# Weight-quarter sums of the up blocks moved from GpSimd to VectorE in a two-layer decoder step

## The reference

```
h2 = rmsnorm(x, g_ffn)                       # 544 x 1024
u, gt = jnp.split(h2 @ w_up, 2, axis=-1)     # 544 x 2816 each
u_ext = jnp.concatenate([conv_buf, u], axis=1)
acc = b_conv
for k in range(CONV_W):                      # CONV_W = 3
    acc = acc + w_conv[k] * u_ext[:, k:k + T]
x = x + (jax.nn.gelu(acc) * gt) @ w_down     # 2816 -> 1024
```

## Time and profile before

| | |
|---|---|
| time, median of 3 runs | 2200.66 us (2198.23 to 2205.04) |
| time of the profiled execution | 2216.76 us |
| its span, first to last instruction | 2214.9 us |
| TensorE matmuls | 2160.3 us busy, 98% |
| VectorE | 1065.3 us busy, 48% |
| ScalarE | 501.3 us busy, 23% |
| GpSimd | 495.9 us busy, 22% |
| mean granted TensorE clock | 0.992 of full |
| DMA | 237.52 MB, 107 GB/s mean |

### The profile page before, as it was taken

The page is one execution under the profiler, slowest core; times in us unless marked ns, Lnnn a source line. Parts: engine busy times, 40 slices in busy tenths (PEclk is TensorE's granted clock), DMA queues, the critical chain, the costliest instruction groups (busy, mean ns, idle before and its releaser), DMA issues.

```text
span 2214.9 us, 30179 instructions
## 1 busy us (share of the span) xinstructions
PE 2160.3 (98%) x12119; PEld 1732.5 (78%) x12119; DVE 1065.3 (48%) x2228; ACT 501.3 (23%) x1076; POOL 495.9 (22%) x501
## 2 busy tenths in 40 slices
PE   8998999999999999999999989999999999999999
PEld 7787866778887888888877867767788878888887
DVE  5466646554115555543326666465441265555522
ACT  3124124432011222210112231354220212222100
POOL 5140010001002443444331300100100034444442
PEclk9999999999999999999999999999999999999999
DMA  5674541112221222222283736210122212222222
GB/s 155 233 249 166 218 153 39 39 41 98 76 80 57 88 84 76 89 78 80 66 286 113 269 120 246 97 39 20 60 98 80 73 60 77 94 77 79 77 85 73
DMA packets 172302, 237.52 MB, mean 107 GB/s; under 512 B 39551, under 2 KB 151680, under 8 KB 169408
## 3 DMA queue, kind: packets, MB, share of 16 engines
q1 hardware_dynamic: 153320, 133.11, 19.6%
q0 software_dynamic: 18400, 102.36, 12.5%
q10 hardware_dynamic: 444, 0.12, 0.0%
HBM read 222.76 MB, written 21.11 MB: 110 GB/s over the span
## 4 chain that ended last, share of the span: by engine, by line
PE 90%; DVE 4%; ACT 2%; DMA 2%; issue 1%; another core or an unknown queue 1%; POOL 0%; DVEq 0%; SPq 0%; ACTq 0%; POOLq 0%
PE PS L918 36%; PE PS L863 27%; PE PS L1029 5%; PE PS L885 4%; PE PS L911 3%; PE PS L1363 2%; PE PS L1280 2%; PE PS L1291 2%; PE PS L429 2%; DMA arena<-in_cache_kv_slc_dram,idx 2%; ACT arena L1574 1%; PE PS L1238 1%; DVE arena L2263 1%; PE PS L1263 1%
## 5 line engine op out<-in xcount | busy, mean ns | idle before, releaser
L863 PE MATMUL PS<-hT,ring 128*128 128x272 f32 x1792 | 425.9, 397 | 5.7 <-issue 2.4
L863 PEld LDWEIGHTS PS<-hT,ring 128*128 128x128 f32 x1792 | 341.5, 192 | 84.7 <-issue 15.2
L1574 ACT ACTIVATE arena<-PS 128x272 f32<-128x272 f32 (+12 forms) x426 | 173.5, 432 | 816.2 <-PE PS L918 221.7
L918 PE MATMUL PS<-arena,ring 128*128 128x272 f32 x1232 | 303.1, 393 | 0.9 <-DVE xT L1932 0.6
L1932 DVE TENSOR_TENSOR arena<-PS,arena 128x272 f32<-128x272 f32 (+4 forms) x204 | 98.7, 493 | 365.4 <-PE PS L918 189.6
L918 PEld LDWEIGHTS PS<-arena,ring 128*128 128x128 f32 x1232 | 233.8, 190 | 49.6 <-issue 1.7
L918 PE MATMUL PS<-arena,kv_kT 128*128 128x272 f32 x912 | 224.3, 395 | 4.4 <-ACT arena L1574 4.4
L815 POOL TENSOR_TENSOR kv_kT<-ring 128x512 f32<-128x512 f32 (+1 forms) x64 | 82.8, 1293 | 607.5 <-PE PS L918 454.9
L1932 DVE TENSOR_TENSOR xT<-PS,xT 128x272 f32<-128x272 f32 (+1 forms) x184 | 85.8, 466 | 267.0 <-PE PS L918 183.5
L918 PEld LDWEIGHTS PS<-arena,kv_kT 128*128 128x128 f32 x912 | 174.2, 191 | 41.3 <-ACT arena L1574 5.3
L863 PE MATMUL PS<-arena,ring 128*128 128x272 f32 x768 | 177.2, 393 | 3.2 <-DVE arena L1932 3.2
(11 more groups left out here) (337 smaller groups left out, 2480.3 us busy)
## 6 DMA issues: line engine op xcount, KB each, us to landing
ring<-in_w_up_dram SPq DMA_DIRECT2D x88, 512.0 KB, 4.5
ring<-in_w_in_dram SPq DMA_DIRECT2D x68, 512.0 KB, 4.5
ring<-in_w_down_dram SPq DMA_DIRECT2D x32, 512.0 KB, 4.4
arena<-in_state_kv_win_dram POOLq DMA_DIRECT2D x4, 2048.0 KB
ring<-in_w_out_dram SPq DMA_DIRECT2D x16, 512.0 KB, 4.0
out_dram<-in_state_kv_win_dram POOLq DMA_DIRECT2D x2, 4064.0 KB, 39.8
ring<-in_w_down_dram SPq DMA_DIRECT2D x16, 384.0 KB, 3.5
ring<-in_w_in_dram SPq DMA_DIRECT2D x16, 256.0 KB, 4.8
```

Source lines behind the costliest of these rows:

```text
L863: mm = pe.matmul(PS[0:m, b + a, 0:HALF], weight(k), rhs(k)[:, HALF * a:HALF * a + HALF], start=(k == 0), stop=(k == nk - 1))
L918: mm = pe.matmul(PS[:, bank, 0:HALF], weight[:, k, :], rhs(k), start=(start and k == 0), stop=(stop and k == kc - 1), skip_group_check=not ...
L1574: return nc.scalar.activation(out, in_, func, **kw)
```

## The change

The sums of u1 to u10 are made by VectorE, in a function of the same four instructions; GpSimd keeps those of g1 to g10 and d0 to d11. The new sums count on a semaphore of their own, `u_sum`, for which TensorE waits in the u blocks. On VectorE the sums of u1 stand after the three copies and ahead of `conv(0)`; those of u_(i+1) stand after `conv(c + 1)` of block i, ahead of the token sums and of the adds of g_i.

```diff
+OTHERS = [name for name in SEVENS if name[0] != "u"]
...
+        def w_summed(eng, name, step):
+
+            if name[0] == "u":
+                return S.at(eng, "u_sum", 4 * int(name[1:]) - 4 + step)
+            return S.at(eng, "w_sum", 4 * OTHERS.index(name) + step)
...
-                for name in SEVENS:
+                for name in OTHERS:
                     weight_sums(name)
...
-                pe.wait_ge(*S.at(pe, "w_sum", 4 * n + 1))
+                pe.wait_ge(*w_summed(pe, name, 1))
...
+                def weight_sums(name):
+
+                    n, s = SEVEN_AT[name], wslot(name)[0]
+                    new = sums[n % 2]
+                    if n >= 2:
+                        dv.wait_ge(*S.filled(dv, last_ticket(SEVENS[n - 2])))
+                    dv.wait_ge(*w_landed(dv, name))
+                    tt(new[:, 0], quarter(s, 4, 0, 1), quarter(s, 4, 1, 1), ALU.add).then_inc(*S.inc(dv, "u_sum"))
+                    tt(quarter(s, 4, 0, 1), quarter(s, 4, 0, 0), quarter(s, 4, 0, 1), ALU.subtract).then_inc(*S.inc(dv, "u_sum"))
+                    dv.wait_ge(*w_summed(dv, name, 1))
+                    tt(new[:, 1], new[:, 0], quarter(s, 4, 0, 0), ALU.subtract).then_inc(*S.inc(dv, "u_sum"))
+                    dv.wait_ge(*w_summed(dv, name, 3))
+                    tt(new[:, 2], quarter(s, 4, 1, 0), new[:, 1], ALU.subtract).then_inc(*S.inc(dv, "u_sum"))
...
+                weight_sums("u1")
                 for c in range(2):
                     conv(c)
...
                     conv(c)
                     conv(c + 1)
+                    if i + 1 < FFN // WCOLS:
+                        weight_sums(f"u{i + 1}")
                     if 4 <= i < 8:
                         for step in range(4):
                             token_sum(i - 4, step)
```

More of the change, by code:

```diff
@@ L815, in weight_sums @@
                     gp.tensor_tensor(new[:, 0], quarter(s, kc, 0, 1), quarter(s, kc, 1, 1), ALU.add).then_inc(*S.inc(gp, "w_sum"))
-                    gp.wait_ge(*S.at(gp, "w_sum", 4 * n + 1))
+                    gp.wait_ge(*w_summed(gp, name, 1))
                     gp.tensor_tensor(quarter(s, kc, 0, 1), quarter(s, kc, 0, 0), quarter(s, kc, 0, 1), ALU.subtract).then_inc(*S.inc(gp, "w_sum"))
                     gp.tensor_tensor(new[:, 1], new[:, 0], quarter(s, kc, 0, 0), ALU.subtract).then_inc(*S.inc(gp, "w_sum"))
-                    gp.wait_ge(*S.at(gp, "w_sum", 4 * n + 3))
+                    gp.wait_ge(*w_summed(gp, name, 3))
                     gp.tensor_tensor(new[:, 2], quarter(s, kc, 1, 0), new[:, 1], ALU.subtract).then_inc(*S.inc(gp, "w_sum"))
-                for name in SEVENS:
+                for name in OTHERS:
                     weight_sums(name)
@@ L933, in seven_products @@
                 pe.wait_ge(*taken[0])
-                pe.wait_ge(*S.at(pe, "w_sum", 4 * n + 3))
+                pe.wait_ge(*w_summed(pe, name, 3))
                 pe.wait_ge(*t2[0])
@@ L941, in seven_products @@
                 pe.wait_ge(*taken[1])
-                pe.wait_ge(*S.at(pe, "w_sum", 4 * n + 4))
+                pe.wait_ge(*w_summed(pe, name, 4))
                 half_product(z, new[:, 2], right, kc, False, True).then_inc(*S.fill(pe, second))
```

## The result

| | before | changed |
|---|---|---|
| median | 2201.45 us (2197.51 to 2205.04, 20 runs) | 2207.72 us (2201.61 to 2213.82, 20 runs) |
| ratio | | 1.0034, 95% interval 1.0026 to 1.0042 |
| span of the profiled execution | 2214.9 us | 2210.8 us |
| VectorE busy | 1065.3 us | 1046.1 us |
| GpSimd busy | 495.9 us | 379.6 us |

The changed kernel is slower by 6.3 us. VectorE got 80 instructions more and is busy 19 us less.

The account below looks back on a forecast made before the run. TensorE was taken to bound blocks u1 to g10. Head delay 5.2 us plus clock 1.7 us gave 6.9 us, on the median of 2200.66 us 2207.6 us, slower by 0.31%; range 2202 to 2212 us.

Parts of the forecast that it names:

- The head delay: Ahead of `conv(0)`: u1's four sums on VectorE delay P3 of u1 by 2.6 us per layer, +5.2 us.
- Nothing for the other blocks: Nine groups per layer on VectorE, 2.6 us each, cost 0, as convolutions beside an idle GpSimd get 3.7 us shorter.
- VectorE too late: Rival at P7 of the gate blocks: convolutions get no shorter, P7 waits, 25 us over both layers, 2233 us; chance 0.06.
- The clock, +1.7 us: TensorE behind the gap ahead of P3 of u1: one half-speed dip more in the first layer, none more in the second.
- The rival with the dearer clock: Behind both gaps ahead of P3 of u1: long clock dips, 8.1 us up to 10 us slower in all; chance 0.14.
- GpSimd's lighter load: GpSimd loses 40 instructions per layer; worth nothing directly, as TensorE never waited for it.
- Meeting GpSimd at the head: u1's new sums beside GpSimd's: 4.3 us more per layer, 8.6 us in all, if they met; taken as 0.
- Faster by a faster engine: Rival ahead of P3 of u1: VectorE's sums in half the time gain at most 2 x 2.2 us, 2196.3 us; chance 0.04.
- 2210.2 us: Whole kernel: the time to which 2 us for the spread of the runs was added, for the range's upper end, 2212 us.
- The side of the line: Whole kernel: forecast 0.31% slower, on the 0.3% a measurement can tell; slower 0.49, same 0.48, faster 0.03.

Follow-up runs that it names:

- e2: The changed kernel with the sums of u1 given back to GpSimd, those of u2 to u10 left on VectorE; ratio 1.0000 to the kernel before.
- e3: The kernel before with only the sums of u1 moved to VectorE, ahead of `conv(0)`; ratio 1.0045 to the kernel before.
- e4: The changed kernel with four further unused additions on VectorE behind the sums of u1; ratio 1.0066 to the kernel before.
- e8: The changed kernel with four unused additions on GpSimd after each block u1 to u9; 2240.28 us, ratio 1.0192 to the kernel before.
- e1: The changed kernel with the sums of u1 moved to behind the activation sums, ahead of the three copies; ratio 1.0005 to the kernel before.
- e6: The changed kernel with ScalarE's copy of P1 of u1 put ahead of gelu of chunk 1; ratio 1.0004 to the kernel before.
- e9: The changed kernel with 16 unused matmuls behind P2 of u1, filling TensorE's gap; ratio 1.0015 to the kernel before.
- e11: The changed kernel run again unedited, on the chip of e9; ratio 1.0047 to the kernel before.
- e7: The changed kernel with u1's sums behind the activation sums and ScalarE's copy of P1 ahead of gelu of chunk 1; ratio 0.9978 to the kernel before.
- e5: The kernel before with ScalarE's copy of P1 of u1 put ahead of gelu of chunk 1; 2193.86 us, ratio 0.9969 to the kernel before.

## Why the prediction was right

**The forecast.** 2207.6 us against 2207.72 us, and +6.9 us against +6.3 us. That the two times meet to 0.1 us is luck: the step is 0.6 us smaller than forecast, and the median of the kernel before rose by 0.8 us from 3 runs to 20. The stretches of the profile give 7.4 us (below). What was right is the mechanism and the size to within 1 us.

**The head delay, +5.2 us: right in size and place.** The four sums took from 700.68 to 703.22 us, 2.54 us (2.56 was worked out), each 0.69 us long. P3 waited 4.74 us (4.8). e2 and e3 show that this is the whole loss, e4 that further delay adds one for one.

**Nothing for the other blocks: right, and for the reason given.** The two convolutions took 4.9 us, as taken from the undisturbed pair, and e8, which takes this relief away, brings the waits of 0.7 and 2.2 us that the rival "VectorE too late" had priced. What that rival had mis-sized is the total, 25 us where e8 measured 32.5: its sum had the waits alone (measured 24.2 us), not the 0.26 us that each of 18 stops costs besides (4.7 us), nor the two dips (3.4 us).

**The clock, +1.7 us: right in kind, 0.6 us small in the profile.** I took +1.7 us for the first layer (bounds 0 and 2.3) and 0 for the second. The profiled executions show +2.3 us in the first and about 0 in the second (1.8 us lost before, 1.7 us now). The two profiled executions of the changed kernel lost 2.3 and 1.7, and 2.1 and 1.7 us, so it pays about 2 us in each layer; the kernel before lost 1.8 us in one of its two layers, and e1, e2 and e6, which have nearly the same gap, 1.6 to 1.7 us in one of theirs. The rival with the dearer clock had the clock cost 2.9 us more than before, and the profile shows 2.2: a dip in both layers, as the forecast had too, but in the second one no longer than before. That it is the clock is what e9 and e11 show: with the gap filled the stretch goes from 278.6 and 278.0 to 276.3 us. Over both layers the stretches add 278.6 + 278.0 - 273.7 - 275.5 = 7.4 us, inside the interval of the ratio (0.26 to 0.42% of 2201.45 us, 5.7 to 9.2 us). How often each gap has a dip in the other runs was not measured.

**GpSimd's lighter load is worth nothing: right.** e7 and e5 have the same stretch.

**Meeting GpSimd at the head: right for the change, and the price was fair.** In e1 three of the four sums took 1.75 us in place of 0.69, 1.06 us more each; 1.07 had been read from the earlier trace rows. In the changed kernel no new sum meets one of GpSimd: all 80 took 0.68 to 0.69 us. The Trainium skill (SBUF — State Buffer, the section on the two separate sides) says that a VectorE instruction with two inputs from SBUF and a GpSimd one that reads SBUF lock each other out for their whole length. e1 agrees in kind: where they meet, VectorE's takes 1.75 us and GpSimd's 1.71 us.

**Faster by a faster engine: fell.** The rule of the Trainium skill (GPSIMD Engine Reference, the table of what to run where) that VectorE is about twice as fast at an elementwise add holds for the instruction, 0.69 against 1.26 us. It made nothing of the time, since TensorE waits for the sums of neither engine.

**Two readings that were loose.** The prediction says that DMA traffic is zero from 695 us on; its own show that only for 695 to 700 us, and 173 GB/s from 705 to 710. What it needed, that the weights of g1 had landed before 695 us, holds: GpSimd began on them at 689.30 us in the changed kernel, set off by their landing. And the 2210.2 us from which the upper end of the range is made stands in no sum of the prediction; its dearest clock, 10 us, would give 2210.7.

**The side of the line.** The forecast lay on 0.3%; the measurement, with an interval from 0.26 to 0.42%, also does. That it is slower is clear, that it is slower by over 0.3% is not.

## What to carry to other kernels

Look at the order of each queue before counting an engine's free time: VectorE was idle for 8.7 us ahead of the three copies, and there the four sums cost nothing (e1), while right behind the copies, 1.35 us after this idle time ended, they were paid one for one. When work moves from one engine to another and the two had slowed each other down, count what the instructions beside it gain: here 2.5 us of new work per block came with 3.7 us of relief. And a wait is often for a queue's order, not for data: moving one copy ahead of an activation on ScalarE was worth 0.31% (e5), about as much as the change lost (0.34%).

## What was not expected of the hardware

- A stop of TensorE costs more than the idle time shown: about 0.26 us more per stop at P7 in e8, and 2.4 us of stretch for a gap of 2.21 us. Where this time goes is not shown.
- Half speed behind a gap does not grow with the gap: behind 4.74 us and 7.64 us the same P3 took 3.99 us in the first layer (in the second 3.49 to 3.79, and 3.99). Behind the 4.74 us it came in all eight cases (the change, e3, e8, e11). Behind 2.2 to 2.3 us it came in one of the two layers of the kernel before, e1, e2 and e6, and in e8 behind 2.2 us in one of the four such stops of each layer.
- GpSimd's sums of g1 started at 689.30 us and met only the last activation sum, where before those of u1 met two; the start was set by the landing of g1's weights. In this meeting GpSimd's instruction was the one that got longer (2.42 us in place of 1.26), and the activation sum kept its 1.28 us; before, both got longer. Nothing waited for it.
